# A hybrid decoder trunk on one core: ordered first loads, a router chain with fewer steps, and matrices loaded behind other readers

## The chip, the cores and the metric

One core of a Trainium2 chip. The metric is the device time of one launch in microseconds (us), the median of the runs shown. The profile is one further execution.

## What is computed

Two layers (`DEPTH = 2`) over 256 tokens of width 1024, all float32:

```python
for l in range(DEPTH):
    h = rmsnorm(x, norm1_g[l])
    proj = h @ w_in[l]                      # 1024 x 2824
    # three mixers side by side on column groups of proj:
    # mLSTM (4 heads), block attention (8 heads), S5 state space (16 groups)
    x = x + concat(y_m, y_a, y_s) @ w_out[l]
    x = x + hierarchical_moe(rmsnorm(x, norm2_g[l]), ...)

def hierarchical_moe(x, ...):               # per token
    g = argmax(x @ w_group + b_group)       # 1 of 4 groups
    top2 of (x @ w_expert + b_expert) inside group g   # 8 experts in a group
    out = sum over both of weight * ((silu(x @ w_gate[e]) * (x @ w_up[e])) @ w_down[e])
```

Each of the 32 experts of a layer has three matrices of 1024 x 512 (2 MB each), so a layer reads 96 matrices, 201 MB. The sum over the experts is the same in whichever order tokens are gathered.

## The kernel before

**Memory.** The ring is 11 tiles of 2 MB in SBUF (`tile(t)`). Matrix n of a layer (n = 0 to 95, six for each pair of experts: gate, gate, up, up, down, down) goes to tile n mod 11. While the mixers run, the same tiles hold the six chunks of `w_in` (tiles 8, 9, 0, 1, 2, 3), `w_out` (tiles 8 and 9) and the mixers' buffers (`qk`, `conv`, `pm`, `decay4`, `so`, `vm` and others), and tile 10 holds the router's buffers (`rt`, `rv`).

**Queues.** SP issues nearly all large DMAs, in one program order, each behind the waits written ahead of it (L509 to L583): first the chunks of `w_in`, then `w_out`, then the first matrices of the layer as the mixers free their tiles (1, 2, 3, 0, 6, then 4, 5, 7 behind `s_mixm` and `s_np`, then 8, 9 behind `s_op`, the last output product), then matrix 10 behind `s_ctl`, in layer 0 ten small loads for the next layer, and from matrix 11 on each pair of loads behind `s_used` of the product that read the tile's last matrix (`tile_free`). ACT's queue starts with the constants, x, four norm gains and ten small rows. POOL issues twelve small parameter loads at the start, and again for layer 1 behind `s_ctl` (L600, L601).

**Start.** PE turns x (`turn_xs`, L1408), DVE and ACT scale it by the gain into `hT`, PE multiplies by chunk 0 (`by_feature`, L1525), then by chunk 1 and so on (`by_token`, L1531). PE waits for `s_cst` (all constants) ahead of everything and for both DMAs of chunk 0 (`s_win[0]` at 32): 1 MB in rows of 1 KB, and 32 KB in 1024 rows of 32 bytes.

**Router.** After the output product PE turns x again (L1408), computes 36 logits for each token (L1824) and keeps itself busy with products that nothing reads (`busy`, L1816). DVE picks group and experts, step by step, each group of instructions closed by a `drain` (L1282 to L1322). PE counts ranks and totals with five products (L1831 to L1835) and puts the residual into four PSUM banks (L1838). DVE finds which tokens are the first 32 of experts 0 and 1 (L1335 to L1343), writes the hit matrix (L857, L860), PE gathers their rows (L1421), ACT copies them to SBUF (L608), PE turns them (L1430), DVE scales them into `xTe` (L849) and the first pass can begin (L1468). Beside this DVE works out the slots of all tokens and the number of passes and writes them to `ctl` (`s_ctl`, L1385). Every engine loads its loop counts from `ctl`.

**Passes.** A pass handles up to 32 tokens of each of two experts: PE does the gate product (L1468), the addition of the pass before (L1440), the up product (L1468), the gather for the next pass (L1421), its turning behind ACT's copy (L1430), and the down product (L1505). A pair of experts has as many passes as its fuller expert needs.

```python
def tile_free(n):                                   # on SP
    m = n - NTILE
    if m % 2 == 0:
        c = C_PASS + 1 + m // 6
        done = sp.value_load(ctl[0:1, c:c + 1], min_val=1, max_val=L * MAXN)
        wait_apart(sp, s_used[kind_of(m)], done)
```

## Time and profile before

| | |
|---|---|
| runs, median (lowest to highest) | 1274.5 us (1273.63 to 1278.43), 3 runs |
| the profiled execution | 1275.59 us |
| its span | 1273.8 us |
| PE busy, share of the span | 1070.6 us, 84% |
| DVE, ACT, POOL busy | 460.3, 180.1, 22.4 us |
| moved by DMA | 440.16 MB, mean 346 GB/s |

The span is from the first to the last instruction; the 1.8 us between it and the execution's own time lie around the program. PE, DVE, ACT, POOL and SP are TensorE, VectorE, ScalarE, GpSimd and SyncE; a q behind a name is the engine's sequencer, which issues DMAs. A float32 matmul appears as two instructions. Matmuls are pipelined, so a busy PE isn't PE at its peak. Idle time of an engine that isn't the bottleneck costs nothing.

### The profile page before, as it was taken

How to read it: one execution, taken by the hardware profiler on the slowest of the kernel's cores; microseconds unless marked ns; L12 is line 12 of the kernel's file. 1: busy time of each engine (PE TensorE's matmuls, PEld its weight loads, DVE VectorE, ACT ScalarE, POOL GpSimd, SP SyncE). 2: the span in 40 equal slices, each digit the busy share in tenths (PEclk: the TensorE clock that was granted, in tenths of full speed). 3: DMA queues.
4: the chain of work that ended last, by engine and by line, in shares of the span. 5: the costliest groups of instructions: out<-in, count | busy, mean ns of one | idle time of the engine just before them, and what ended most of it. 6: DMA issues, size and time to landing. Idle time of an engine off the chain costs nothing.

```text
span 1273.8 us, 22730 instructions
## 1 busy us (share of the span) xinstructions
PE 1070.6 (84%) x9476; PEld 578.6 (45%) x9476; DVE 460.3 (36%) x1253; ACT 180.1 (14%) x427; POOL 22.4 (2%) x34
## 2 busy tenths in 40 slices
PE   5999999999967777776799999899677777679977
PEld 4476655454533333333355755554333333334533
DVE  0786345433322222222247753533222222224331
ACT  2314310010100000000024161100000000000100
POOL 3000002000000000000000000000000000000000
PEclk9999999999988888888899999999888888889998
DMA  9711379999999999999993313899999999997996
GB/s 313 261 71 67 132 291 355 389 428 426 430 427 427 425 428 429 427 427 427 391 339 141 133 67 132 353 387 428 427 427 427 426 428 427 428 427 327 427 426 278
DMA packets 50660, 440.16 MB, mean 346 GB/s; under 512 B 9320, under 2 KB 12040, under 8 KB 25488
## 3 DMA queue, kind: packets, MB, share of 16 engines
q1 hardware_dynamic: 48672, 436.33, 83.1%
q0 software_dynamic: 800, 0.99, 0.5%
q10 hardware_dynamic: 1104, 1.59, 0.4%
q8 instruction: 69, 1.13, 0.4%
q14 instruction: 15, 0.12, 0.0%
HBM read 437.31 MB, written 1.05 MB: 344 GB/s over the span
## 4 chain that ended last, share of the span: by engine, by line
PE 55%; DMA 40%; DVE 2%; issue 1%; DVEq 1%; ACT 0%; ACTq 0%; SPq 0%
DMA ring<-in_e_w_up_dram 39%; PE PS L1468 12%; PE PS L1531 9%; PE PS L1505 7%; PE PS L1767 4%; PE PS L1430 4%; PE PS L1421 4%; PE PS L1525 3%; PE PS L1440 2%; PE PS L1701 1%; PE PS L1721 1%; PE PS L1481 1%; DMA gT<-in_norm_g_dram 1%; PE PS L1657 1%; PE PS L1824 1%
## 5 line engine op out<-in xcount | busy, mean ns | idle before, releaser
L1468 PE MATMUL PS<-ring,hT 128*32 128x256 f32 x4608 | 336.6, 452 | 164.1 <-DMA ring<-in_e_w_gate_dram 107.7
L1468 PEld LDWEIGHTS PS<-ring,hT 128*32 128x32 f32 x4608 | 181.8, 125 | 339.6 <-issue 275.9
L1505 PE MATMUL PS<-ring,hT 128*32 128x512 f32 x1152 | 134.2, 607 | 8.5 <-issue 8.2
L880 DVE TENSOR_SCALAR hT<-hT 128x256 f32<-128x256 f32 x36 | 11.0, 306 | 302.4 <-ACT hT L613 302.4
L1531 PE MATMUL PS<-ring,hT 128*128 128x512 f32 x256 | 114.8, 602 | 0.0
L1430 PE MATMUL PS<-cst,ring 64*64 64x64 f32 x1216 | 81.2, 282 | 5.8 <-ACT ring L608 1.4
L1430 PEld LDWEIGHTS PS<-cst,ring 64*64 64x64 f32 x1216 | 77.0, 212 | 15.1 <-issue 11.9
L887 DVE TENSOR_TENSOR hT<-hT,PS 128x256 f32<-128x256 f32 x36 | 15.2, 422 | 174.7 <-PE PS L1468 174.7
L1421 PE MATMUL PS<-xres,scr 128*64 128x512 f32 x304 | 73.6, 605 | 0.0
L1531 PEld LDWEIGHTS PS<-ring,hT 128*128 128x128 f32 x256 | 48.1, 193 | 54.7 <-issue 54.6
L608 ACT COPY ring<-PS 128x512 f32<-128x512 f32 x38 | 22.3, 587 | 352.6 <-PE PS L1421 352.6
L1440 PE MATMUL PS<-hT 64*128 64x512 f32 x288 | 71.8, 615 | 0.0
L1505 PEld LDWEIGHTS PS<-ring,hT 128*32 128x32 f32 x1152 | 36.0, 111 | 77.1 <-issue 75.4
L882 DVE RECIPROCAL hT<-hT 128x256 f32<-128x256 f32 x36 | 63.1, 1753 | 2.6
L1767 PE MATMUL PS<-ring 128*128 128x512 f32 x128 | 58.1, 602 | 1.9 <-DVE ring L1268 1.9
L618 ACT COPY hT<-PS 128x512 f32<-128x512 f32 x36 | 21.1, 586 | 215.5 <-PE PS L1505 215.5
L613 ACT ACTIVATE hT<-PS 128x256 f32<-128x256 f32 x36 | 13.8, 384 | 266.3 <-PE PS L1468 266.3
L849 DVE TENSOR_TENSOR hT<-PS,gT 128x512 f32<-128x512 f32 x38 | 26.3, 692 | 69.0 <-PE PS L1430 69.0
L1525 PE MATMUL PS<-hT,ring 128*128 128x256 f32 x192 | 44.9, 394 | 2.3 <-ACT hT L631 2.3
L889 DVE COPY hT<-PS 128x256 f32<-128x256 f32 x36 | 15.3, 425 | 74.8 <-PE PS L1485 74.8
L1525 PEld LDWEIGHTS PS<-hT,ring 128*128 128x128 f32 x192 | 37.8, 199 | 8.7 <-issue 3.4
L1440 PEld LDWEIGHTS PS<-hT 64*128 64x128 f32 x288 | 25.5, 186 | 32.4 <-issue 32.4
(341 smaller groups left out, 901.9 us busy)
## 6 DMA issues: line engine op xcount, KB each, us to landing
ring<-in_e_w_gate_dram SPq DMA_DIRECT2D x64, 2048.0 KB, 41.2
ring<-in_e_w_up_dram SPq DMA_DIRECT2D x64, 2048.0 KB, 44.0
ring<-in_e_w_down_dram SPq DMA_DIRECT2D x60, 2048.0 KB, 42.7
ring<-in_w_in_dram SPq DMA_DIRECT2D x10, 2048.0 KB, 18.8
ring<-in_w_out_dram SPq DMA_DIRECT2D x2, 4096.0 KB, 13.1
ring<-in_e_w_down_dram SPq DMA_DIRECT2D x8, 1024.0 KB, 39.5
...
```

Source lines behind the costliest of these rows:

```text
L608: act.copy(rows_g, PS[:, 0, :]).then_inc(gs, 1)
L618: act.copy(Y, PS[:, 3, :]).then_inc(s_ys, 1)
L849: V.tensor_tensor(xTe, PS[:, 0, :].rearrange("p (k s) -> p k s", k=KD), bcast(gT[:, l, 1, :], PAIR), ALU.mult).then_inc(xte, 1)
L882: V.reciprocal(es, es)
L1421: last = pe.matmul(PS[64 * h:64 * h + 64, 0, :], hit[:, j, :], xres[:, j, 512 * h:512 * h + 512], start=j == 0, stop=j == NT - 1)
L1430: last = pe.matmul(PS[r, 0, PAIR * k:PAIR * k + PAIR], rows_g[r, k::KD], ident[r, r], start=True, stop=True)
L1440: pe.matmul(PS[:, 4 + 2 * j + h, :], hitT[r, j, :], Y[r, :], start=False, stop=False)
L1468: last = pe.matmul(PS[o:o + UT, bank, 0:256], xTe[:, k, UT * u:UT * u + UT], w[u][:, k, :, 2 * h:2 * h + 2], start=k == 0, stop=k == KD - 1)
L1505: last = pe.matmul(PS[o:o + UT, 3, :], hTe[:, c % 2, hc:hc + UT], w[u][:, c, 512 * h:512 * h + 512], start=c == 0, stop=c == KF - 1)
L1525: last = pe.matmul(PS[:, bank, T * half:T * half + T], wchunk(c)[:, k, col:col + P], hT[:, k, :], start=k == 0, stop=k == KD - 1)
L1531: last = pe.matmul(PS[:, bank, :], hT[:, k, P * j:P * j + P], wchunk(c)[:, k, 0:512], start=k == 0, stop=k == KD - 1)
L1767: last = pe.matmul(PS[:, OUT_BANK[n], :], mixT[:, k, P * j:P * j + P], wout[:, k, 512 * h:512 * h + 512], start=k == 2, stop=k == 1)
```

## The change

Three parts.

**First loads.** ACT's queue now issues the first norm gain, the identity (the first 128 columns of the constants), x, chunk 0 of `w_in`, and the rest of the constants. SP issues the ten small rows of group 0, waits for x, then chunks 1 to 5, the other three gains and the rest. POOL's parameters wait for x too. PE and ACT wait for the identity, the gain and the rest of the constants where they use them, and PE runs four products on ones that DVE writes at the start.

**Router.** The group logits are written straight to their padded buffer, the argument of the group's exponentials is written one step later, the ranks need two products (a zero block ahead of the masks, `mks`, gives both token halves at once) and the totals two more behind them, the first hits are found with two steps in place of five, and three of the four residual products take the place of the filler products. `ctl` is written before the slots of all tokens; the slots and the weights come after `xTe`, and end in a new semaphore `s_rtd`. ACT copies the gathered rows block by block (`by_feature` to `by_block`: it now reads PSUM at a stride of 8 elements and PE reads SBUF without one), for the first pair in two halves, and PE turns them in halves in two banks, behind `s_ctl` and its own loads from `ctl`; the gate product waits for the second half before its fifth step. The copy of every later pass reads PSUM in the same way.

**Matrices.** Matrix 7 is issued behind `s_dp` (the last decay product), 5 behind `s_pm`, 4 behind `s_hmT`; matrix 10 behind `s_rtd`, with the ten small loads behind it.

The diff, cut (lines of context left out; what it removes of the second half of DVE's routing stands in the kernel above, L1324 to L1385):

```diff
-    for c0, n in CH[c]:
-        sp.dma_start(wchunk(c)[:, :, a:a + n], at(win_v, l)[0, :, :, c0:c0 + n]).then_inc(s_win[c], 16)
-        a += n
-for c in range(6):
-    load_chunk(c, 0)
+load_small(sp, 0, (0,))
+sp.wait_ge(s_x, 16)
+for c in range(1, 6):
+    load_chunk(sp, c, 0)
+for l, gi in ((0, 1), (1, 0), (1, 1)):
+    load_gain(sp, l, gi).then_inc(s_gain, 16)
...
     load_matrix(l, 6)
-    sp.wait_ge(s_mixm, l + 1)
+    sp.wait_ge(s_dp, MH * l + MH)
+    load_matrix(l, 7)
+    sp.wait_ge(s_pm, MH * l + MH)
+    load_matrix(l, 5)
+    sp.wait_ge(s_hmT, l + 1)
     load_matrix(l, 4)
-    load_matrix(l, 5)
-    sp.wait_ge(s_np, MH * l + MH)
-    load_matrix(l, 7)
...
     load_matrix(l, 9)
-    wait_apart(sp, s_ctl, l + 1)
...
 def _(pool):
+pool.wait_ge(s_x, 16)
...
         if n == 0:
-            act.wait_ge(s_gain, 32 * L)
+            act.wait_ge(s_gain0, 16)
+        elif n == 1:
+            act.wait_ge(s_gain, 16 * (2 * L - 1))
...
     act.drain()
+    if n == 0:
+        act.wait_ge(s_cst, 16)
...
-act.dma_start(cst[:, :], consts[:, 0:NC]).then_inc(s_cst, 16)
+load_gain(act, 0, 0).then_inc(s_gain0, 16)
+act.dma_start(cst[:, 0:C_MQK], consts[:, 0:C_MQK]).then_inc(s_id, 16)
 act.dma_start(xres[:, :, :], x_v).then_inc(s_x, 16)
...
-load_small(act, 0, (0,))
+load_chunk(act, 0, 0)
+act.dma_start(cst[:, C_MQK:], consts[:, C_MQK:NC]).then_inc(s_cst, 16)
 act.preload_act_table_set("natural_log_exp_and_others")
-act.wait_ge(s_cst, 16)
...
     act.activation(dif, dif, ACT.Exp).then_inc(s_rve, 1)
-    rows_gathered(s_gath0, s_gs0, l)
+    act.wait_ge(s_gath0, l + 1)
+    for c in range(2):
+        act.copy(by_block(rows_g)[:, 4 * c:4 * c + 4, :], by_feature(PS[:, 0, :])[:, 4 * c:4 * c + 4, :]
+                 ).then_inc(s_gs0, 1)
...
 V = nc.vector
+V.memset(mixT[:, 0:2, :].rearrange("p k t -> p (k t)"), 1.0).then_inc(s_warm, 1)
...
     n = 2 * l + gi
-    dve.wait_ge(s_gain, 32 * L)
+    if n == 0:
+        dve.wait_ge(s_gain0, 16)
+    else:
...
+    V.memset(gl8, -3.0e38)
+    V.memset(mks[:, 0, :], 0.0)
+    V.drain()
...
     for j in range(NT):
-        V.scalar_tensor_tensor(lg[:, j, :], PS[:, 0, 64 * j:64 * j + 36], rs[:, j:j + 1], rb[:, :], ALU.mult,
-                               ALU.add)
-    V.memset(gl8, -3.0e38)
-    V.drain()
-    V.tensor_copy(gl8[:, :, 0:4], lg[:, :, 0:4])
+        V.scalar_tensor_tensor(gl8[:, j, 0:4], PS[:, 0, 64 * j:64 * j + 4], rs[:, j:j + 1], rb[:, 0:4],
+                               ALU.mult, ALU.add)
+    for j in range(NT):
+        V.scalar_tensor_tensor(lg[:, j, :], PS[:, 0, 64 * j + 4:64 * j + 36], rs[:, j:j + 1], rb[:, 4:36],
+                               ALU.mult, ALU.add)
...
         V.max_index(idx[:, 0, j, :], gmx[:, j, :], gl8[:, j, :])
-    V.tensor_tensor(pex, lg[:, :, 0:4], gmx[:, :, 0:1].broadcast_to([P, NT, 4]), ALU.subtract).then_inc(s_rg, 1)
...
     V.tensor_tensor(elp, gid, gsel.broadcast_to([P, NT, NE]), ALU.not_equal)
-    V.drain()
-    V.scalar_tensor_tensor(elp, elp, NEG, lg[:, :, 4:36], ALU.mult, ALU.add)
+    V.tensor_tensor(pex, gl8[:, :, 0:4], gmx[:, :, 0:1].broadcast_to([P, NT, 4]), ALU.subtract).then_inc(s_rg, 1)
+    V.drain()
+    V.scalar_tensor_tensor(elp, elp, NEG, lg, ALU.mult, ALU.add)
...
     V.tensor_copy(eid, idx[:, 1, :, 0:2])
-    dve.wait_ge(s_rge, l + 1)
-    V.tensor_reduce(pgs, pex, X, ALU.add)
-    V.drain()
-    V.reciprocal(pgs, pgs)
+    V.drain()
...
     V.drain()
-    V.tensor_tensor(mks, mk[:, 0], mk[:, 1], ALU.add).then_inc(s_mk, 1)
+    V.tensor_tensor(mks[:, 1:], mk[:, 0], mk[:, 1], ALU.add).then_inc(s_mk, 1)
+    V.memset(Y, 0.0)
+    V.memset(hitT, 0.0)
+    V.drain()
+    ranks = PS[:, 1, 0:64].rearrange("p (j n) -> p j n", j=NT)
+    dve.wait_ge(s_rk, l + 1)
+    V.scalar_tensor_tensor(fsh, ranks[:, :, 0:2], 1.0, mks[:, 1:, 0:2], ALU.add, ALU.mult)
+    V.drain()
+    for j in range(NT):
+        for u in range(2):
+            last = V.tensor_scalar(hit[:, j, UT * u:UT * u + UT], cst[:, C_T + 1:C_T + 1 + UT], fsh[:, j, u:u + 1],
+                                   rs[:, j:j + 1], ALU.is_equal, ALU.mult)
+    last.then_inc(s_hit0, 1)
+    dve.wait_ge(s_cn, l + 1)
+    nf = nu.rearrange("p i u -> p (i u)")
+    V.tensor_scalar(nf, PS[:, 2, 0:NE], 1.0, 1.0 / UT, ALU.max, ALU.mult)
+    V.tensor_copy(rnk, ranks)
+    V.drain()
+    V.tensor_scalar(nf, nf, 31.0 / 64, ROUND, ALU.add, ALU.add)
+    V.tensor_scalar(fr32, rnk, 1.0 / UT, -31.0 / 64, ALU.mult, ALU.add)
+    V.drain()
+    V.tensor_scalar(nf, nf, -ROUND, None, ALU.add)
+    V.drain()
+    V.tensor_tensor(npass, nu[:, :, 0], nu[:, :, 1], ALU.max)
+    V.drain()
+    V.tensor_tensor_scan(pend, cst[:, C_ONES:C_ONES + NPAIR], npass, 0.0, ALU.mult, ALU.add)
+    V.tensor_copy(ctl[:, C_NP:C_NP + NPAIR], npass[0:1, :])
+    V.tensor_copy(c_p0, past[:, 0:1])
+    V.drain()
+    V.tensor_scalar(upr, pend[0:1, :], past[:, 0:1], None, ALU.add)
+    V.tensor_copy(c_tot, pend[0:1, NPAIR - 1:NPAIR])
+    V.drain()
+    V.tensor_copy(ctl[:, C_PASS + 1:C_PASS + 1 + NPAIR], upr).then_inc(s_ctl, 1)
+    V.tensor_copy(past[:, 0:1], upr[:, NPAIR - 1:NPAIR])
+    for c in range(2):
+        dve.wait_ge(s_rT0, 2 * l + c + 1)
+        V.tensor_tensor(xTe[:, 4 * c:4 * c + 4, :], PS[:, (3, 0)[c], 0:256].rearrange("p (k s) -> p k s", k=4),
+                        bcast(gT[:, l, 1, 4 * c:4 * c + 4], PAIR), ALU.mult).then_inc(s_xte0, 1)
+    V.tensor_scalar(fr32, fr32, ROUND, -ROUND, ALU.add, ALU.add)
+    V.tensor_tensor(pst[:, :, 0], pend, npass, ALU.subtract)
+    V.drain()
+    V.scalar_tensor_tensor(rnk, fr32, float(UT), rnk, ALU.mult, ALU.add)
+    V.tensor_scalar(pst[:, :, 1], pst[:, :, 0], float(PAIR), float(UT), ALU.mult, ALU.add)
+    V.tensor_scalar(pst[:, :, 0], pst[:, :, 0], float(PAIR), None, ALU.mult)
+    V.drain()
+    V.tensor_tensor(rnk, rnk, rv[:, 160:192].unsqueeze(1).broadcast_to([P, NT, NE]), ALU.add)
+    dve.wait_ge(s_rge, l + 1)
+    V.tensor_reduce(pgs, pex, X, ALU.add)
+    V.drain()
+    for a in range(2):
+        V.tensor_tensor(rtm[:, a], mk[:, a], rnk, ALU.mult)
+    V.reciprocal(pgs, pgs)
...
     V.drain()
+    V.tensor_reduce(sh.rearrange("p a j -> p (a j)"), rtm.rearrange("p a j n -> p (a j) n"), X, ALU.add)
...
     V.drain()
+    V.tensor_copy(sw, sh)
...
     V.drain()
-    V.tensor_tensor(wgt[:, :, 1:2], wgt[:, :, 0:1], dif, ALU.mult)
-    V.memset(Y, 0.0)
-    V.memset(hitT, 0.0)
...
+    V.tensor_tensor(wgt[:, :, 1:2], wgt[:, :, 0:1], dif, ALU.mult).then_inc(s_rtd, 1)
+    V.drain()
...
-    pe.wait_ge(s_xte0, l + 1)
+    pe.wait_ge(s_xte0, 2 * l + 1)
...
 pe.sem_inc(s_xte, 1)
-pe.wait_ge(s_cst, 16)
+pe.wait_ge(s_warm, 1)
+warm = mixT[:, 0:2, :].rearrange("p k t -> p (k t)")
+for n in range(4):
+    pe.matmul(PS[:, 4 + n % 2, :], warm[:, 0:P], warm, start=True, stop=True)
+pe.wait_ge(s_id, 16)
...
         for k in range(KD):
+            if kind == 0 and k == KD // 2:
+                pe.wait_ge(s_xte0, 2 * l + 2)
...
-    def busy(n):
-        for k in range(n):
-            pe.matmul(PS[:, 4 + 2 * (k % 2), :], ident, cst[:, 0:512], start=True, stop=True)
     turn_xs(l, 1)
-    busy(1)
...
-    busy(4)
+    def residual(n):
+        pe.matmul(PS[:, 4 + n, :], ident, xres[:, n // 2, 512 * (n % 2):512 * (n % 2) + 512], start=True, stop=False)
+    for n in range(3):
+        residual(n)
     pe.wait_ge(s_mk, l + 1)
+    flat_mks = mks.rearrange("p j n -> p (j n)")
     bef = cst[:, C_BEFORE:C_BEFORE + P]
-    pe.matmul(PS[:, 1, 0:NE], bef, mks[:, 0, :], start=True, stop=True)
-    pe.matmul(PS[:, 1, NE:2 * NE], ones, mks[:, 0, :], start=True, stop=False)
-    pe.matmul(PS[:, 1, NE:2 * NE], bef, mks[:, 1, :], start=False, stop=True)
-    pe.matmul(PS[:, 1, 2 * NE:3 * NE], ones, mks[:, 0, :], start=True, stop=False)
-    pe.matmul(PS[:, 1, 2 * NE:3 * NE], ones, mks[:, 1, :], start=False, stop=True).then_inc(s_rk, 1)
-    for j in range(NT):
-        for h in range(2):
-            pe.matmul(PS[:, 4 + 2 * j + h, :], ident, xres[:, j, 512 * h:512 * h + 512], start=True, stop=False)
+    pe.matmul(PS[:, 1, 0:2 * NE], bef, flat_mks[:, NE:3 * NE], start=True, stop=False)
+    pe.matmul(PS[:, 1, 0:2 * NE], ones, flat_mks[:, 0:2 * NE], start=False, stop=True).then_inc(s_rk, 1)
+    pe.matmul(PS[:, 2, 0:NE], ones, mks[:, 1, :], start=True, stop=False)
+    pe.matmul(PS[:, 2, 0:NE], ones, mks[:, 2, :], start=False, stop=True).then_inc(s_cn, 1)
+    residual(3)
...
     gather(s_gath0)
-    pe.wait_ge(s_gs0, l + 1)
-    turn_gathered(s_rT0)
-    wait_apart(pe, s_ctl, l + 1)
+    pe.wait_ge(s_ctl, l + 1)
+    passes = pe.value_load(ctl[0:1, C_NP:C_NP + 1], min_val=1, max_val=MAXN // 2)
+    past_n = pe.value_load(ctl[0:1, C_PASS:C_PASS + 1], min_val=0, max_val=L * MAXN)
+    for c in range(2):
+        pe.wait_ge(s_gs0, 2 * l + c + 1)
+        for k in range(4 * c, 4 * c + 4):
+            for h in range(2):
+                r = slice(64 * h, 64 * h + 64)
+                last = pe.matmul(PS[r, (3, 0)[c], PAIR * (k % 4):PAIR * (k % 4) + PAIR],
+                                 by_block(rows_g)[r, k, :], ident[r, r], start=True, stop=True)
+        last.then_inc(s_rT0, 1)
```

## Rows read from the trace of the kernel before

**Rows 1.** The page, 40 slices: GB/s

```profile
GB/s 313 261 71 67 132 291 355 389 428 426 430 427 427 425 428 429 427 427 427 391 339 141 133 67 132 353 387 428 427 427 427 426 428 427 428 427 327 427 426 278
```

**Rows 2.** Timeline 0 to 60: start, us, engine, line, operation, idle before and releaser

```profile
9.96 3.65 PE L1408 MATMUL PS<-cst,xres 128*128 128x128 f32 x16 [9.96 <-DMA xres<-in_x_dram]
...
13.80 1.06 ACT L628 ACTIVATE scr<-xres 128x1024 f32<-128x1024 f32 x1 [4.50 <-DMA gT<-in_norm_g_dram]
...
17.27 9.39 PE L1525 MATMUL PS<-hT,ring 128*128 128x256 f32 x32 [1.44 <-ACT hT L631]
```

**Rows 3.** DMA issues of the whole run: KB each, median us to landing

```profile
cst<-in_consts_dram ACTq DMA_DIRECT2D x1, 484.5 KB, 3.6
```

**Rows 4.** Line L521, the issue at 1.5 us (second DMA of chunk 0)

```profile
DMA to landing us min/median/max: 14.7/14.7/14.7
```

**Rows 5.** DMA queues from 5 to 8 us: packets, MB, share (q10 ACT, q1 SP)

```profile
q10 hardware_dynamic: 218, 0.83, 70.9%
q1 hardware_dynamic: 218, 0.22, 21.3%
```

**Rows 6.** DMA queues from 16 to 26 us

```profile
q1 hardware_dynamic: 1937, 3.90, 105.1%
```

**Rows 7.** The chain that ended last, 70 to 90 us

```profile
79.34 6.91 PE PS L1525 x32
```

**Rows 8.** Timeline of PE, 340 to 392 us

```profile
378.46 6.24 PE L1468 MATMUL PS<-ring,hT 128*32 128x256 f32 x64 [5.67 <-DMA ring<-in_e_w_gate_dram]
...
388.48 3.83 PE L1468 MATMUL PS<-ring,hT 128*32 128x256 f32 x64 [1.86 <-DMA ring<-in_e_w_up_dram]
```

**Rows 9.** Timeline 172 to 225, layer 0: router chain to the first pass

```profile
190.66 0.23 DVE L1322 TENSOR_TENSOR ring<-ring 128x64 f32<-128x64 f32 x1
...
192.08 3.68 PE L1838 MATMUL PS<-xres,cst 128*128 128x512 f32 x8
...
192.41 0.10 DVE L1336 TENSOR_TENSOR ring<-PS,cst 128x4 f32<-128x4 f32 x1
...
194.32 0.29 DVE L860 TENSOR_TENSOR scr<-scr 128x128 f32<-128x128 f32 x1
...
195.69 1.94 PE L1421 MATMUL PS<-xres,scr 128*64 128x512 f32 x8
...
197.67 0.59 ACT L608 COPY ring<-PS 128x512 f32<-128x512 f32 x1 [7.67 <-PE PS L1421]
...
198.31 2.14 PE L1430 MATMUL PS<-cst,ring 64*64 64x64 f32 x32 [0.69 <-ACT ring L608]
...
199.09 0.15 DVE L1385 CAST ctl<-ring 1x16 int32<-1x16 f32 x1
199.27 0.33 SPq L516 DMA_DIRECT2D ring<-in_e_w_down_dram  x1
...
200.82 0.69 DVE L849 TENSOR_TENSOR hT<-PS,gT 128x512 f32<-128x512 f32 x1 [1.58 <-PE PS L1430]
...
201.76 3.83 PE L1468 MATMUL PS<-ring,hT 128*32 128x256 f32 x64 [1.32 <-DVE hT L849]
...
203.72 0.25 SPq L477 DMA_DIRECT2D small<-in_s_glu_b_dram  x1
```

**Rows 10.** Line L516, issue at 205.7 us (matrix 11)

```profile
DMA to landing us min/median/max: 11.7/11.7/11.7
```

**Rows 11.** Line L516, issue at 241.1 us (matrix 17)

```profile
DMA to landing us min/median/max: 8.1/8.1/8.1
```

**Rows 12.** Window: PE, PEld, DVE, ACT, POOL busy, PEclk, DMA share, GB/s

```profile
206.00:212.00 6.00, 6.00 (x76) 2.63 (x74) 3.33 (x4) 0.04 (x1) 1.81 (x3) 1.00 1.05 273
```

**Rows 13.** Timeline 804 to 845, layer 1: matrices 10 and 11, first pass

```profile
824.65 8.12 SPq L516 DMA_DIRECT2D ring<-in_e_w_down_dram  x2
...
826.88 5.46 PE L1468 MATMUL PS<-ring,hT 128*32 128x256 f32 x64 [1.41 <-DVE hT L849]
```

**Rows 14.** Line L516, issues at 832.4 and 832.8 us (matrices 11, 12, layer 1)

```profile
DMA to landing us min/median/max: 8.1/10.3/12.6
```

More of the change, by code:

```diff
@@ L323, in build @@
         s_rk = sem("ranks_ready")
+        s_cn = sem("counts_ready")
         s_ctl = sem("units_ready")
+        s_rtd = sem("routing_buffers_read")
         s_out = sem("stored")
@@ L860, in row_hits @@
                 V.tensor_tensor(hit, hit3[:, 0], hit3[:, 1], ALU.add).then_inc(ready, 1)
-            def hits(ready):
-                row_hits(ready, iota, sh)
                 V.tensor_scalar(sh, sh, -float(PAIR), None, ALU.add)
```

90 lines of the change are left out of this document (37 added, 53 removed).

## The prediction

> **What bounds the kernel.** Read the slices first [rows 1]: DMA runs at 427 GB/s for most of the time and is nearly idle in two valleys, while the mixers run. The ring holds 11 matrices, so outside the valleys the time is bytes by rate: a 2.1 MB matrix takes 2.1/0.427 = 4.9 us. So three things can shorten it: a mixer that begins earlier, less idle DMA between a mixer and the steady stream, or fewer small packets within it. A faster instruction elsewhere is worth nothing.
>
> **The start.** In the timeline [rows 2] PE turns x from 9.96 (it waited for x). ACT starts only at 13.80, held by the norm gains, the first product starts at 17.27 behind `hT`. From there PE leads the chain through the mixer, so what the first product gains, the mixer's end and all behind it gain. Two more things are to be seen. Both queues progress packet for packet: 218 against 218 between 5 and 8 us [rows 5], although ACT's are four times as large. And the first product is slow: 9.39 us, where the same 32 instructions take 6.91 later [rows 7], so 2.5 are lost to a slow clock. After 5.67 us of idling a gate product took 6.24 us, after 1.86 only 3.83 [rows 8].
>
> *x.* The constants, first in the queue, landed 3.6 us after issue [rows 3]: 0.5 MB at 390 GB/s (3.90 MB in 10 us [rows 6]) is 1.3, so 2.3 go before the data flows. x, 1.05 MB, takes 2.7; issued third at about 1.7, overlapping that latency, it lands at some 6.4 (now 9.96, when PE went on [rows 2]). ACT's square (1.06) and scalings, and PE's turning (3.65 [rows 2]) bring `hT` to about 11.
>
> *Chunk 0.* Its second DMA, 1024 rows of 32 bytes, landed at 1.5 + 14.7 = 16.2 [rows 4], so it was barely hidden already. Now its first DMA runs alone behind x (1.05 MB, 2.8 us, to 9.2), but SP issues chunk 1 when x lands, and that reaches the engines at 9.2 or a little later (a lone matrix lands 8.1 us after issue, 3.2 more than its 4.9 [rows 11]). From then the tiny rows alternate with 2 KB packets, which go at 1937/10 = 194 in a us [rows 6]. If all 1024 alternate, 5.3 us and their own cost: landing at 15.5 to 17.5, POOL's small packets included. If a good part slips ahead, 12 to 13. I take 14.3, between them, since chunk 1 can't begin earlier than SP's wait allows. The product starts at 14.5: 2.8 earlier. Of the 2.5 of slow clock I take 0.8 back: PE idles 3 to 4 us between its turning and the product, between the two gaps of [rows 8]. **Start: -3.6**, bounds +1 (17.5 and more, no clock) and -8.7 (`hT` at 11 leads, clock kept). The rest of the constants comes behind chunk 0, at about 17; first needed by the scales, long ahead of the product on ones after the gate columns. Covered by the first product; uncovered it would cost what it is late. Chunks 1 to 5 keep their rate and are used later than they land.
>
> **The router, layer 0** [rows 9]. Masks ready at 190.9. The copy, one reduction, one reciprocal and two drains leave the path, two narrow logit writes come in: -0.35, to 190.55. Ranks need two products before their signal in place of five, each pair 0.22: ready at 191.4 (DVE resumed at 192.4). The clearing of `Y` and `hitT`, between L1322 and L1336, now lies beside them. First hits: DVE took 2.2 us (192.4 to 194.6); two steps and four writes take 1.3, to 192.7. The residual products, which held the gather until 195.69 although the hits were there at 194.61, are done by then, as three ran while DVE chose experts. Gather at 192.8 (-2.9), done at 194.75. The path to `ctl`: 14 groups took 4.5 us behind the hits (to 199.1), 0.32 each; seven are left: 195.0. PE then loads its counts. No row shows that by itself; DVE went from 199.24 to 200.82 with two such loads and a wait for PE that ended at 200.45, so it lies between 0 and 1.6; I take 1.2, near the upper end, since DVE started late after its releaser. Turning 196.2 to 198.4 (2.14), second half of `xTe` 198.8. The pass starts at 198.4 in place of 201.76: -3.4.
>
> That isn't what the time follows, though. Matrix 10, issued at 199.27, now waits for `s_rtd`: seven groups, 15 instructions, behind `xTe`, 2.8 us by the same price (bounds 2.3 and 3.3): 201.6, so it is issued 2.4 **later**. Queued behind it on SP are ten small loads (the last issued at 203.72, 0.25 us: 4.7 us in all after matrix 10) and only then the wait for tile 0: matrix 11 is issued at about 206.3 (now 205.7), though the gate product ends at 202.3. Matrix 10 alone would land at 209.7, 11 at 214.6. POOL's small loads wait for `ctl` alone, as matrix 10 did, and start some 4.2 us earlier. They cost the stream dearly: 273 GB/s from 206 to 212 [rows 12] is (427-273) x 6/427 = 2.2 us, and matrix 11 landed 11.7 after issue [rows 10] in place of 8.1. Moved ahead they fall half into time in which DMA idles: 1.6 us of loss are left, 11 lands at 216.2 (now 217.4), matrix 16 at 241.2. Matrix 17 was issued at 241.1 only (pair 1 needs two passes) and landed 8.1 later [rows 11], at 249.2. With the passes 3.4 ahead it is issued at 237.7, and lands behind 16: 246.2. I take **-2.6** for layer 0, bounds 0 and -3.4 (the passes' own lead). From there DMA is never idle, and the layer's end moves with it.
>
> **Layer 1** [rows 13]. Matrix 10 was issued at 824.65, 11 at 832.43 behind the gate product, and landed 8.1 later, at 840.5 (the first of the two in [rows 14]). Now 10 at 827.1, landed 835.2, 11 behind it 840.1; the gate product (at the latest 829) isn't last any more. **-0.4**, bounds +1 and -2.
>
> **Matrices 4, 5, 7.** They move ahead by 1 to 10 us, but 8 and 9 still wait for the last output product, and 10 for the router. The stream then idles for some 10 us ahead of matrix 10. Worth nothing: what the first pass reads has landed anyhow. SP's waits in front of them end in the order written. The filler products take no time that anyone waits for; their cover, keeping PE's clock, is taken by residual products.
>
> **The strided copy.** ACT copies 512 columns in 0.59 us in each pass [rows 9]; no row shows PSUM read at a stride. PE has transposes to do while it runs (the first copy of a layer has no such cover). I take no change; at twice the price it adds 0.5 us in the last pass of each layer and in the first ones; below zero nothing, as it reads the same bytes.
>
> The Trainium skill ("SBUF — State Buffer", section "Door 1: The DMA port swizzle") says that PSUM comes in lines of 8 bytes and that "any non-contiguous PSUM access pattern significantly slows down matmuls". It names no figure for a copy. By it the sum would be smaller by some 1 to 2 us; no row here shows it.
>
> **Sum:** -3.6 - 2.6 - 0.4 = -6.6. The profiled execution took 1275.6 and comes to 1269.0; against the median of 1274.5, 1.1 below it, 1267.9. Half a per cent (6.4 us) is about what a measurement of this kernel can tell from no change.
>
> **Rivals.**
> *A, the tiny rows stay last.* Chunk 0 lands at 16.5 to 18, the start gives 0 to 0.8. For it: 218 against 218. Against: its first DMA has 2.8 us alone behind x. Then -0.5 - 2.6 - 0.4: 1271.0. Chance 0.27. The Trainium skill ("DMA: Bandwidth & Descriptors", section "Rules for kernel authors") says that spreading DMAs over queues doesn't help bandwidth, as all share 16 engines; by that, only the order counts, which would be this case.
> *B, chunk 0 lands by 11 and PE keeps its clock.* Start -8, sum -11: 1263.5. For it: the rows of 32 bytes are small. Against: the gap of 5.67 in [rows 8]. Chance 0.16.
> *C, slower: matrix 10 behind a longer chain.* If the strided halves cost three times their 0.59/2 and the loads from `ctl` 1.6, `s_rtd` comes 2.5 us later still: 10 lands at 837.7 in layer 1, 11 at 842.6 (+2.1), in layer 0 the small loads and 11 slip by as much (0 left of the gain), the last passes add 1 each, and if the start gives nothing either the sum is +4: 1278.5. It decides from `s_rtd` later than 827.4 in layer 1. For it: the stream idles in both layers at this point. Chance 0.07.
> That the change doesn't do what it says at the start, since another of PE's waits (`s_par`) ends as late, would look like A and is in its chance.
>
> **Chances.** The forecast 0.5; C 0.07, A 0.27, B 0.16. Of the forecast's own spread (1264 to 1271) some two thirds lie beyond -6.4: faster 0.33 + 0.16 + 0.02 = 0.51; same 0.17 + 0.25 + 0.01 = 0.43; slower 0.06. The range takes A in and most of B: 1261.5 to 1273.5.
>
> **What would show it.** Right: x landed by 6.5, first product at 13 to 16; first pass 3 to 4 us earlier after the logits; matrix 10 issued later after the logits than now, matrix 17 issued before 16 has landed; DMA idle before matrix 10; matrices 4, 5, 7 earlier without effect. Wrong: chunk 0's second DMA the last before the product and later than 17, a copy L608 over 0.8 us, or matrix 11 of layer 1 landing longer after its matrices 8 and 9 were issued than now.

## The result, and the profile after

The kernel after takes 1261.2 us (median of 4 runs, 1258.8 to 1264.6); before, run beside it, takes 1276.5 (1273.6 to 1286.9). **The ratio is 0.9873, interval 0.9848 to 0.9898.** The same file measured once more, later, gave 0.9900 (0.9872 to 0.9929); the two say 16 and 13 us faster. The forecast was 6.6 us faster, 1267.9, with a range down to 1261.5: the sign was right, and the gain was at least twice as large.

The profiled execution took 1264.6 (span 1262.8, 11.0 below that of before). DMA of the page in 40 slices, and the granted clock:

```profile
PEclk9999899999988888888899999899888888789988
...
GB/s 308 275 103 55 119 390 271 428 426 428 426 429 424 429 427 429 426 427 429 381 343 141 134 67 206 261 417 427 427 426 427 427 427 428 428 426 362 428 427 284
```

The shape is that of [rows 1], with the two valleys. Outside them the slice that stands out is the fourth from the right, late in layer 1: it was 327 and is 362. Nothing in the prediction touched it.

**The start.** Timeline of the kernel after (start, length, engine, line, operation, count, idle before):

```profile
6.94 2.03 PE L1437 MATMUL PS<-cst,xres 128*128 128x128 f32 x16
...
9.29 2.15 ACT L653 ACTIVATE hT<-PS,gT 128x128 f32<-128x128 f32 x8
...
11.69 8.83 PE L1560 MATMUL PS<-hT,ring 128*128 128x256 f32 x32 [2.04 <-ACT hT L653]
```

The first product waits for ACT's half of `hT`, not for chunk 0, and starts at 11.69 in place of 17.27 [rows 2]. Where chunk 0's two DMAs (1 KB rows, then the 1024 rows of 32 bytes) landed, by the issues of their line:

```profile
L521 ACTq DMA_DIRECT2D ring<-in_w_in_dram x2: 637/659/681, 2.1 to 2.8; - x2
...
DMA to landing us min/median/max: 7.6/7.7/7.9
```

Issued at 2.15 and 2.81, landed at 10.0 and 10.4: the tiny rows landed only 0.4 us behind the large ones.

**The router, layer 0**, same view (it answers to [rows 9]):

```profile
178.94 3.81 PE L1854 MATMUL PS<-rw,hT 128*128 128x36 f32 x32 [0.27 <-ACT hT L653]
...
192.99 1.15 PE L1883 MATMUL PS<-cst,ring 64*64 64x64 f32 x32 [1.62 <-ACT ring L838]
...
194.39 3.88 PE L1499 MATMUL PS<-ring,hT 128*32 128x256 f32 x64 [0.25 <-DVE hT L1387]
...
197.28 0.33 SPq L536 DMA_DIRECT2D ring<-in_e_w_down_dram  x1
```

From the end of the logits (182.75; before 186.04) to the first pass it is 11.6 us in place of 15.7. Matrix 10 is issued at 197.28, 14.5 behind the logits in place of 13.2. Matrix 17, which ends the stage for DMA:

```profile
L536 SPq DMA_DIRECT2D ring<-in_e_w_down_dram x1: 340/340/340, 231.8 to 231.8; - x1
...
DMA to landing us min/median/max: 11.8/11.8/11.8
```

It lands at 243.6. Counted from the turning of x for the router (176.57; before 179.46) that is 67.1 us in place of 69.7. In layer 1:

```profile
816.85 3.83 PE L1499 MATMUL PS<-ring,hT 128*32 128x256 f32 x64 [0.25 <-DVE hT L1387]
...
819.99 1.52 SPq L536 DMA_DIRECT2D ring<-in_e_w_down_dram  x2
```

Both issues stand in one row: 10 at 819.99, 11 at 821.19. Matrix 11 no longer waits for the gate product but queues behind 10, and lands at 833.5 (before 840.5 [rows 14]).

**The turning of the gathered rows**, which the prediction had used as a duration and not as a term. Groups by line (busy us, mean ns of one; before, the group also holds the first pass of each layer, which the kernel after has on a line of its own). First before:

```profile
L1430 PE MATMUL PS<-cst,ring 64*64 64x64 f32 x1216 | 81.2, 282 | 5.8 <-ACT ring L608 1.4
L1430 PEld LDWEIGHTS PS<-cst,ring 64*64 64x64 f32 x1216 | 77.0, 212 | 15.1 <-issue 11.9
L608 ACT COPY ring<-PS 128x512 f32<-128x512 f32 x38 | 22.3, 587 | 352.6 <-PE PS L1421 352.6
```

Then the kernel after:

```profile
L1459 PE MATMUL PS<-cst,ring 64*64 64x64 f32 x1152 | 41.3, 220 | 4.4
L1459 PEld LDWEIGHTS PS<-cst,ring 64*64 64x64 f32 x1152 | 37.4, 134 | 11.9 <-issue 11.9
L628 ACT COPY ring<-PS 128x512 f32<-128x512 f32 x36 | 21.1, 585 | 324.9 <-PE PS L1450 324.9
```

Per pass, 32 of these took 2.14 us and now take 1.15. The weights of the products are the gathered rows: before, PE loaded every 8th column (`rows_g[r, k::KD]`), now a contiguous block. ACT reads at the stride instead, and its copy took 585 ns against 587.

### The profile page after: what moved, and what is told of

It reads as the page before. It is cut to its first block, busy times and chain, and to the rows that moved or that the text cites. A ratio compares the mean times of both kernels' runs of the same rounds, so it can differ in the third digit from the quotient of the medians.

```text
span 1262.8 us, 22686 instructions
## 1 busy us (share of the span) xinstructions
PE 1041.1 (82%) x9460; PEld 546.6 (43%) x9460; DVE 458.5 (36%) x1246; ACT 180.0 (14%) x429; POOL 22.3 (2%) x34
## 4 chain that ended last, share of the span: by engine, by line
PE 52%; DMA 43%; issue 2%; DVE 1%; ACT 1%; ACTq 1%; SPq 0%; DVEq 0%
DMA ring<-in_e_w_up_dram 36%; PE PS L1499 11%; PE PS L1566 9%; PE PS L1536 6%; PE PS L1803 5%; DMA ring<-in_e_w_gate_dram 4%; PE PS L1560 3%; PE PS L1450 3%; DMA ring<-in_e_w_down_dram 3%; PE PS L1459 2%; PE PS L1469 2%; PE PS L1737 1%; PE PS L1757 1%; PE PS L1512 1%; PE PS L1693 1%
## 5 line engine op out<-in xcount | busy, mean ns | idle before, releaser
L1499 PE MATMUL PS<-ring,hT 128*32 128x256 f32 x4608 | 340.6, 456 | 171.8 <-DMA ring<-in_e_w_gate_dram 124.9
L1499 PEld LDWEIGHTS PS<-ring,hT 128*32 128x32 f32 x4608 | 185.6, 126 | 348.1 <-issue 287.8
L906 DVE TENSOR_SCALAR hT<-hT 128x256 f32<-128x256 f32 x36 | 10.6, 294 | 346.1 <-ACT hT L633 345.8
L1536 PEld LDWEIGHTS PS<-ring,hT 128*32 128x32 f32 x1152 | 38.3, 112 | 95.9 <-issue 94.9
L1803 PE MATMUL PS<-ring 128*128 128x512 f32 x128 | 60.8, 625 | 1.9 <-DVE ring L1293 1.9
L1459 PE MATMUL PS<-cst,ring 64*64 64x64 f32 x1152 | 41.3, 220 | 4.4
L1459 PEld LDWEIGHTS PS<-cst,ring 64*64 64x64 f32 x1152 | 37.4, 134 | 11.9 <-issue 11.9
L1803 PEld LDWEIGHTS PS<-ring 128*128 128x128 f32 x128 | 24.9, 201 | 29.1 <-issue 26.3
```

Of the source, the lines that this page charges most:

```text
L1459: last = pe.matmul(PS[r, 0, PAIR * k:PAIR * k + PAIR], by_block(rows_g)[r, k, :], ident[r, r], start=True, stop=True)
L1499: last = pe.matmul(PS[o:o + UT, bank, 0:256], xTe[:, k, UT * u:UT * u + UT], w[u][:, k, :, 2 * h:2 * h + 2], start=k == 0, stop=k == KD - 1)
L1536: last = pe.matmul(PS[o:o + UT, 3, :], hTe[:, c % 2, hc:hc + UT], w[u][:, c, 512 * h:512 * h + 512], start=c == 0, stop=c == KF - 1)
L1803: last = pe.matmul(PS[:, OUT_BANK[n], :], mixT[:, k, P * j:P * j + P], wout[:, k, 512 * h:512 * h + 512], start=k == 2, stop=k == 1)
```

## The experiments

One table serves all of them. It cuts the profiled execution of each kernel at events on the path, in us: from the first product's start (F) to the first turning for the router (T0), to matrix 17's landing, and so on; "starved" is the time between the landings of layer 1's matrices 76 and 77 (the 175th and 176th expert load, as two matrices of a layer come in halves), "last" from the last landing to the end.

| kernel | F | mixer 0 | T0 to 17 | last load to layer 1 | mixer 1 | T1 to 17 | starved | last |
|---|---|---|---|---|---|---|---|---|
| before | 17.3 | 162.2 | 69.7 | 10.4 | 159.1 | 65.7 | 10.5 | 11.3 |
| after | 11.7 | 164.9 | 67.1 | 9.2 | 159.0 | 64.6 | 8.1 | 10.3 |
| turning back | 11.7 | 161.5 | 67.3 | 9.2 | 161.0 | 63.3 | 10.6 | 11.3 |
| turning alone | 18.0 | 160.8 | 68.3 | 9.2 | 160.1 | 65.8 | 8.0 | 10.3 |
| start back | 18.4 | 165.3 | 66.8 | 9.8 | 165.3 | 63.3 | 7.8 | 10.3 |
| start, turning | 11.8 | 159.6 | 69.6 | 9.8 | 159.1 | 64.0 | 7.8 | 9.3 |
| chunk 1 early | 21.4 | 162.8 | 67.2 | 9.2 | 164.1 | 63.6 | 7.8 | 10.3 |
| tiny rows first | 13.5 | 163.0 | 67.2 | 9.4 | 159.1 | 64.5 | 7.9 | 9.3 |
| no warm-up | 12.3 | 163.5 | 66.8 | 9.7 | 165.3 | 63.5 | 9.3 | 9.3 |
| after again | 12.0 | 161.6 | 67.7 | 9.2 | 164.2 | 63.7 | 8.3 | 10.2 |
| order back | 11.7 | 160.4 | 66.7 | 9.8 | 159.1 | 64.8 | 8.3 | 10.3 |
| filler back | 12.1 | 160.4 | 67.4 | 9.2 | 159.0 | 64.7 | 8.0 | 10.3 |
| own buffers | 11.7 | 159.9 | 64.3 | 9.2 | 160.9 | 59.4 | 8.1 | 10.3 |
| own buffers, small loads | 11.8 | 160.4 | 64.0 | 9.2 | 160.8 | 59.4 | 8.0 | 10.3 |

The parts left out are the same in all: 386.3 to 386.5 from matrix 17 to layer 0's last load, 291.7 to 291.8 from 17 to 76 in layer 1, 89.5 to 89.8 from 77 to the end of the loads. That is the stream whose time is bytes by rate. Both mixers vary by up to 6 us between executions and follow no edit that one profile each can show. The other columns also move by 0.5 to 1.5 us where no edit touches them, so a difference of that size in one row shows nothing by itself.

### The turning back, and the turning alone

```diff
-                act.copy(by_block(rows_g), by_feature(PS[:, 0, :])).then_inc(gs, 1)
+                act.copy(rows_g, PS[:, 0, :]).then_inc(gs, 1)
-                        last = pe.matmul(PS[r, 0, PAIR * k:PAIR * k + PAIR], by_block(rows_g)[r, k, :], ident[r, r], start=True,
+                        last = pe.matmul(PS[r, 0, PAIR * k:PAIR * k + PAIR], rows_g[r, k::KD], ident[r, r], start=True,
```

> The kernel after, with the passes' copy and turning as before: ACT copies the gathered rows as they lie, PE turns every 8th column (the first pass of a layer keeps the new form, since its halves are copied apart). Theory T (contiguous weights shorten each pass by 1 us where a pass is on the path: end of layer 0 1.0, a starved stretch late in layer 1 2.3, last pass 1.1): the turning group takes 2.1 us again in place of 1.15, and the time is 4.4 us above the kernel after, 1265.6, ratio to before 0.9915. Rival (the turning lies beside the stream of matrices and is worth nothing; the eleven microseconds are start and router): the group is slower but the time stays at 1261.2, ratio 0.988.

Measured: ratio 0.9919 (0.9891 to 0.9946), 1266.0 us. That is 2 us above the kernel after by its second ratio and 6 by its first, and the intervals of all three overlap: the time alone doesn't settle it. Its groups:

```profile
L1459 PE MATMUL PS<-cst,ring 64*64 64x64 f32 x1152 | 76.9, 282 | 4.4
L1459 PEld LDWEIGHTS PS<-cst,ring 64*64 64x64 f32 x1152 | 73.0, 212 | 12.0 <-issue 12.0
```

Where it counts is seen around the starved stretch. Windows (us, PE busy, clock, DMA share, GB/s), first of before:

```profile
1150.00:1160.00 10.00, 9.87 (x120) 1.00 0.87 369
1160.00:1170.00 10.00, 10.00 (x147) 1.00 0.47 167
```

after:

```profile
1150.00:1160.00 10.00, 10.00 (x146) 1.00 0.63 228
1160.00:1170.00 10.00, 9.88 (x132) 1.00 1.01 429
```

and with the turning back:

```profile
1140.00:1150.00 10.00, 9.88 (x120) 1.00 0.86 367
1150.00:1160.00 10.00, 10.00 (x148) 1.00 0.49 169
```

A pair with three passes keeps its matrices three passes long, and SP issues no load meanwhile: DMA has landed all it was given and waits, PE is full. Before, matrix 77 was issued at 1164.8, 2.4 us after 76 had landed at 1162.4; after, at 1154.4, 0.3 before 76 landed. With the turning back the gap is there again (issue at 1154.65, 76 landed at 1152.3).

The gap has two causes, though, and the turning is one. In the first of the three passes the down product was slow in both kernels that show the gap of 2.4, and fast in the kernel after. Before, then after:

```profile
1138.07 5.27 PE L1505 MATMUL PS<-ring,hT 128*32 128x512 f32 x32 [1.24 <-issue]
```

```profile
1130.36 3.64 PE L1536 MATMUL PS<-ring,hT 128*32 128x512 f32 x32 [0.52 <-issue]
```

The run without the warm-up (below) has the new turning and that slow product:

```profile
1134.99 5.30 PE L1535 MATMUL PS<-ring,hT 128*32 128x512 f32 x32 [2.15 <-issue]
...
L536 SPq DMA_DIRECT2D ring<-in_e_w_down_dram x1: 328/328/328, 1160.7 to 1160.7; - x1
```

The granted clock was 0.83 there from 1130 to 1140, and 1.00 in the kernel after. Matrix 76 had landed at 1159.4, so the gap was 1.3: at the same slow product, the turning closes 1.0 of the 2.4, and "starved" is 9.3 in place of 10.5. The rest goes with the clock. Both kernels with the old turning had the slow product and eleven of the twelve with the new one had not; whether the shorter turning or chance moves the slow stretch is open.

The other place is the last pass, after:

```profile
1250.81 1.15 PE L1459 MATMUL PS<-cst,ring 64*64 64x64 f32 x32
1251.89 3.64 PE L1536 MATMUL PS<-ring,hT 128*32 128x512 f32 x32
```

and with the turning back:

```profile
1250.95 2.14 PE L1459 MATMUL PS<-cst,ring 64*64 64x64 f32 x32
1253.02 3.64 PE L1536 MATMUL PS<-ring,hT 128*32 128x512 f32 x32
```

So by the columns the turning is worth 1.2 + 1.0 = 2.2 us with the clock taken out, and 3.4 with it. The expectation had put 1.0 more at the end of layer 0, and that fell: "last load to layer 1" is 9.2 with the turning back too. ("Last" is 9.3 in three runs with the new turning: there the granted clock stayed at full in the 14 us before the last load landed, where it fell to half for 3.4 us in all the others.)

> The kernel before, with the copy by blocks and the turning of contiguous columns alone, nothing else changed. Theory T: 4.4 us below before, 1272.1, ratio 0.9965, turning group 1.15 us, ACT copy of 512 columns still 0.59 us. Rival (off the path): 1276.5, ratio 1.000.

Measured: 0.9976 (0.9958 to 0.9993), 1274.0 beside 1277.5 of before. The group is at 1.15 us, the copy at 585 ns, starved 8.0, last 10.3. The rival (worth nothing) is out by the interval, narrowly, and by both columns; the size is 3 us by the ratio, 1 to 5 by its interval. Here the turning also counts in layer 0: matrix 17 waits for the passes there, and from the end of the first gate product to its issue it is 33.5 us in place of 35.5. In the kernel after, 17 is issued before 16 has landed, and "T0 to 17" is the same with the turning back. So the worth of the parts doesn't add up, and of the 2.7 that "T0 to 17" fell from before to after, the turning alone gives 1.4.

### The start

> The kernel after, with the loads at the start in the order of before (constants ahead of x, the norm gains behind it, all chunks on SP) and without the four products on ones. Theory S (what the first product gains is kept to the end): first product at 17.3 us, time 6.1 above the kernel after, 1267.3, ratio 0.9928. Rival G (the mixer gives 3.4 us of it back by a lower granted clock at 130 to 160 us, as in the one profile of the kernel after, whenever it begins earlier): 2.7 above, 1263.9, ratio 0.990.

Edit: the `load_*` calls of the three DMA queues in the order of before, and no products on ones. Measured: 0.9938 (0.9919 to 0.9956), 1270.0. First product at 18.4, a microsecond later than before, as x landed at 12.8 and not at 9.8. The time is 5 to 8 us above the kernel after by its two ratios, for a first product 6.7 us later: theory S. Both mixers took 165.3 here, though they began late, so rival G's dip needs no early beginning. The first product took 7.15 us, with the loads of before and no warm-up:

```profile
18.36 7.15 PE L1552 MATMUL PS<-hT,ring 128*128 128x256 f32 x32 [0.49 <-ACT hT L648]
```

> The kernel before, with the new start and the new copy and turning, but the router, its residual products and the order of matrices 4, 5, 7 as before. Theory (start 6.1, turning 4.4, all kept but for dips of the clock that fall differently in each run): 1276.5 - 10.5 = 1266.0, ratio 0.992, and what is left to the kernel after, 3 to 5 us, is the router's. Rival G (2.7 for the start): 1269.4, ratio 0.9945, and the router is worth 8.

Measured: 0.9924 (0.9903 to 0.9945), 1267.2. What is left to the kernel after is 0.0024 to 0.0051 by its two ratios, 3 to 6 us, as the theory had it; the columns "T0 to 17" and "T1 to 17" say some 2 and nothing. With the router of before this run has 64.0 in layer 1, as short as the new router's 63.3 to 64.8. Its gate product there:

```profile
818.40 3.83 PE L1492 MATMUL PS<-ring,hT 128*32 128x256 f32 x64 [0.98 <-DVE hT L874]
```

Before took 5.46 [rows 13] and the turning alone 5.43, and these two have the 65.7 and 65.8: that a new router shortens layer 1 isn't shown.

> The kernel after, unchanged. Theory D (the mixers' length varies from execution to execution with the granted clock, by up to 5 us, and the profile of the kernel after had caught a dip in layer 0): the time from the first product to the turning of x for the router, 164.9 us in that profile, is between 159 and 165, the stream of matrices behind it repeats to 0.3 us, ratio to before 0.987 to 0.990. Rival (the new kernel always pays 3.4 us in layer 0's mixer): again 164.9 within 0.5.

Measured: 0.9900 (0.9872 to 0.9929), 1265.7 beside 1278.2. The mixer of layer 0 took 161.6 and not 164.9; layer 1's took 164.2 and not 159.0. Windows over 130 to 150 us, first of the kernel after, then again:

```profile
130.00:150.00 20.00, 20.00 (x70) 0.80 0.07 17
```

```profile
130.00:150.00 20.00, 20.00 (x81) 0.95 0.16 50
```

The granted clock was 0.80 there in the one and 0.95 in the other, the same program. Theory D holds: the dip in the first profile of the kernel after, which hid 2.7 us of its gain (F to T0 took 164.9 against 162.2 of before), belongs to the execution.

### Chunk 0 and its tiny rows

Edit: SP does not wait for x before chunks 1 to 5.

```diff
             load_small(sp, 0, (0,))
-            sp.wait_ge(s_x, 16)
```

> The kernel after, with SP not waiting for x before chunks 1 to 5: chunk 1 is issued at about 4.6 us in place of 6.8. Theory I (a row of 32 bytes takes a turn of its own beside each 2 KB packet of another queue, and in the kernel after they were only spared because chunk 1 was not yet flowing): chunk 0's second DMA lands at 14 us or later in place of 10.4, the first product starts 3 us later, 1264.5, ratio to before 0.990. Rival (the tiny rows are cheap even beside other packets): lands by 12, first product by 12.5, time within 1 us of the kernel after, 0.988.

Measured: 0.9958 (0.9937 to 0.9979), 1274.3, which is 7 to 11 us above the kernel after. The same view of chunk 0's two DMAs, and the first product:

```profile
L521 ACTq DMA_DIRECT2D ring<-in_w_in_dram x2: 637/659/681, 2.1 to 2.8; - x2
...
DMA to landing us min/median/max: 9.2/13.8/18.5
```

and in the timeline

```profile
21.41 9.46 PE L1559 MATMUL PS<-hT,ring 128*128 128x256 f32 x32 [11.74 <-DMA ring<-in_w_in_dram]
```

The tiny rows landed at 2.8 + 18.5 = 21.3, 11 us later than in the kernel after, for an issue of chunk 1 that was 2.0 us earlier. Theory I has the mechanism and undershot the size. Chunk 1 itself (1024 rows of 2 KB, on SP's queue) landed at 18.0, so the 1024 tiny rows were spread over the whole of it and the beginning of chunk 2: one of theirs for each large one, as the 218 against 218 of [rows 5] had it. The queues from 11 to 13 us here (packets, MB, share), then ACT's in the kernel after from 9 to 10:

```profile
q1 hardware_dynamic: 302, 0.62, 88.0%
...
q10 hardware_dynamic: 301, 0.01, 10.7%
```

```profile
q10 hardware_dynamic: 971, 0.24, 133.2%
```

That is 150 tiny rows in a microsecond beside the large ones, and over 870 where only ACT's queue moved.

In the second variant ACT also issues the tiny rows ahead of the 1 KB rows:

> As the run in which SP issues chunk 1 without waiting for x (there chunk 0's 1024 rows of 32 bytes landed at 21.3 us), but ACT issues the rows of 32 bytes ahead of chunk 0's rows of 1 KB. Theory I (what counts is how many rows take a turn beside the 2 KB packets, whatever their size, and the tiny ones now go before chunk 1 flows): the tiny rows land by 9 us, the 1 KB rows, alternating with chunk 1, by 13 to 16, the first product starts by then and not at 21.4; time 0.991 to 0.993 of before. Rival (chunk 1 takes the engines whatever the order): both land at 20 or later, first product at 20, ratio 0.9955.

Measured: 0.9905 (0.9873 to 0.9937), 1264.3.

```profile
L521 ACTq DMA_DIRECT2D ring<-in_w_in_dram x2: 637/659/681, 2.1 to 2.8; - x2
...
DMA to landing us min/median/max: 5.8/8.2/10.6
```

and in the timeline

```profile
13.53 9.76 PE L1558 MATMUL PS<-hT,ring 128*128 128x256 f32 x32 [3.60 <-DMA ring<-in_w_in_dram]
```

The tiny rows landed at 7.9, 0.8 us behind x, and the 1 KB rows, now those that share the engines with chunk 1, at 13.4. Theory I again, in both landings (the ratio came out a little better than the 0.991 to 0.993 expected, within its interval). So the 32-byte rows cost what stands beside them, not what they carry.

The Trainium skill says in "DMA: Bandwidth & Descriptors", section "Queues, rings and completion order", that each DMA engine goes round the queues it has work for, a packet at a time. The trace agrees: 301 packets of ACT's queue went beside 302 of SP's.

### The products on ones

> The kernel after, without the four products on ones ahead of the identity. Theory W (they matter only through PE's clock in the first turning): the turning of x takes 3.6 us in place of 2.0, the first product starts 1 to 2 us later, time 1.5 above the kernel after, ratio 0.9885. Rival (they also carry the clock into the first product): that product takes 9.4 or more in place of 8.8, and the time is 2.5 above.

Measured: 0.9892 (0.9852 to 0.9932), 1266.6.

```profile
7.13 3.65 PE L1436 MATMUL PS<-cst,xres 128*128 128x128 f32 x16 [7.13 <-DMA xres<-in_x_dram]
```

The turning took 3.65 again, in place of 2.03, as theory W said, but the product started at 12.3, only 0.6 later in place of 1 to 2: ACT's scalings of `hT` are the last to end. It took 8.67, in this one profile. With the warm-up the same product took 7.14 four times and 8.8 four times where it began by 12.1, so nothing shows what the warm-up does for it. The time can't be told from the kernel after's.

### Order of matrices 4, 5, 7, and the filler

> The kernel after, with matrices 4, 5, 7 issued in the order and behind the waits of before. Theory O (worth nothing, as matrices 8 and 9 and then 10 wait for later events and DMA idles between them): the time from the turning of x for the router to the landing of matrix 17 is 67.0 us in layer 0 as in the kernel after, ratio 0.987 within its interval. Rival (matrices 8 and 9 land later and hold up the first pass's up product or push matrix 10): 17 lands a microsecond or more later after the turning, ratio above 0.989.

Measured: 0.9899 (0.9861 to 0.9936), 1263.3, the ratio of the repeated kernel after; T0 to 17 is 66.7, no later. Worth nothing that can be told, as theory O had it.

> The kernel after, with one filler product (512 columns) put back between the turning of x and the router's products. Theory F (it is on the path since hT is ready as soon as the turning ends, contrary to the prediction's sentence on fillers): the router's products end 6.6 us after the turning began, as before, in place of 6.2, in both layers. Rival (DVE's and ACT's copies of hT hide it, as predicted): 6.2, unchanged.

Measured, one run, which says nothing of the time: 1260.7. The timeline shows the filler, two entries of 1.02 us together, between the turning (at 172.51) and the logits:

```profile
174.45 1.02 PE L1850 MATMUL PS<-cst 128*128 128x512 f32 x2
175.31 3.94 PE L1855 MATMUL PS<-rw,hT 128*128 128x36 f32 x32
```

The logits end 6.7 us after the turning began (6.1 in the repeated kernel after), and the first pass starts 18.4 after it and not 17.8. In layer 1 they end at 6.5, between the 6.7 and 6.1 of the two profiles of the kernel after, so layer 0 alone supports it. Theory F holds there: the filler was on the router's path. Yet "T0 to 17" is 67.4, within what the kernel after gives (67.1 and 67.7), so its 0.6 us did not reach the stream that can be told.

### The router's buffers outside the ring

In the kernel after, matrix 10 waits for `s_rtd`, because the router's buffers lie in its tile. Here they lie in the idle part of hT and of the scratch:

```diff
-        rt = so[:, :, :].rearrange("p j n -> p (j n)")
-        rv = vm[:, 0:512]
+        rt = work[:, 1536:2048]
+        rv = scr[:, 640:1024]
+        rs8 = scr[:, 384:400]
+        rmk = scr[:, 400:496]
...
                 load_matrix(l, 9)
-                sp.wait_ge(s_rtd, l + 1)
                 load_matrix(l, 10)
+                wait_apart(sp, s_ctl, l + 1)
...
+                act.wait_ge(s_rtd, l + 1)
                 wait_apart(act, s_ctl, l + 1)
```

(`rs8` and `rmk` hold `gl8` and `mks`; their clearing comes behind the wait for `s_rs`.)

> The kernel after, with the router's buffers outside the ring (the idle part of hT and of the scratch), so that matrix 10 is issued right behind 8 and 9 and waits for no router; ACT waits for the router's last step ahead of its first pass. Theory B (in the kernel after matrix 10, issued only when the router ends, sets when matrix 11 lands in layer 1, and POOL's small loads and the gate product do in layer 0): matrix 10 lands by 196 in layer 0; 11 is issued when the first gate product ends; layer 1's matrix 11 lands 8.1 us after issue, 4 us earlier; layer 0 gains 0.5 to 2. Time 5 below the kernel after, 1256.2, ratio to before 0.9835. Rival (the passes' own speed sets layer 1, DMA soon catches up with the last readers of the ring): no more than 1 below the kernel after, 0.987.

Measured: **0.9822 (0.9791 to 0.9853), 1255.8 us**, 6 to 10 us below the kernel after by its two ratios. Matrix 11's issue in layer 0 and in layer 1:

```profile
L538 SPq DMA_DIRECT2D ring<-in_e_w_down_dram x1: 350/350/350, 193.4 to 193.4; - x1
...
DMA to landing us min/median/max: 11.2/11.2/11.2
...
L538 SPq DMA_DIRECT2D ring<-in_e_w_down_dram x1: 328/328/328, 813.6 to 813.6; - x1
...
DMA to landing us min/median/max: 8.8/8.8/8.8
```

In layer 1 it lands 8.8 after issue in place of 12.3, and T1 to 17 falls from some 64 to 59.4; in layer 0 T0 to 17 falls from 67 to 64.3. Theory B, with the 5 us it gave come out at 7: matrix 10 landed at 190.5 in layer 0 (by 196 expected), and layer 0 gained 2.8 or more (0.5 to 2 expected).

> As the run with the router's buffers outside the ring, and the next layer's small loads (SP's behind matrix 10, POOL's behind the logits) are issued while DMA is idle under the router. Theory B2 (the small packets cost the stream about 1.6 us where they lie beside matrices 11 and 12): layer 0's matrix 11 lands 8.1 us after issue in place of 9.9; 1.5 to 2 us below the run with the buffers alone, 1254.5, ratio 0.982. Rival (their cost is hidden since the passes set the pace at that point): equal to that run.

Measured: 0.983 (0.9798 to 0.9862), 1256.1: equal to the run before, so the rival holds. Matrix 11 does land 8.5 us after issue in place of 11.2:

```profile
L538 SPq DMA_DIRECT2D ring<-in_e_w_down_dram x1: 350/350/350, 194.5 to 194.5; - x1
...
DMA to landing us min/median/max: 8.5/8.5/8.5
```

But T0 to 17 gains 0.3 only: matrix 17 can't be issued before the second pass of its pair, and was at 228.0, 0.8 us before 16 landed.

## Why the prediction was right and wrong

By the two profiles, the 11.0 us of span are: start -5.6, mixer 0 +2.7, router of layer 0 -2.7, end of layer 0 -1.2, router of layer 1 -1.1, starved stretch -2.3, last pass -1.0, and +0.2 in the streams. Without the mixer, whose length belongs to the execution, that is -13.7, or 0.989 of before, between the two measured ratios. Three more of these parts are not the edit's alone: about half of the starved stretch goes with a lower clock, the 1.2 at the end of layer 0 are there with the turning back too, and the 1.1 of layer 1 are there with the router of before (64.0 in "start, turning"). That the total comes out between the ratios doesn't show the parts.

**What bounds the kernel.** "Outside the valleys the time is bytes by rate" holds for 768 us of the span and fails in the slice of 327 GB/s of [rows 1], which lay in plain view; no reason for it was sought. "A faster instruction elsewhere is worth nothing" was drawn from it, and **this is the step that failed**: the pass sets the pace behind a pair with three passes and at the end, and a shorter turning counts there. It put at nothing what made the time 3 us shorter when it was done alone (1 to 5 by its interval).

**The strided copy.** The sum took "no change" for ACT's side, which was right (585 ns against 587), and stopped there. The other side of the same edit, PE reading contiguous weights in place of every 8th column, was never priced, although [rows 9] had the 2.14 us for 32 products and the sum used them for the new kernel's first pass too. The sentence of the Trainium skill that the prediction quotes ("SBUF — State Buffer", section "Door 1: The DMA port swizzle") is about matmuls. For ACT's copy the trace shows no such price: it reads 512 columns at a stride of 8 in the same time.

For the weights, the trace has 212 ns a load at a stride of 8 and 134 ns contiguous, 64 columns. The Trainium skill gives in "TensorE: Matmul & The Clock Gate", section "LDWEIGHTS (loading the stationary operand)", a time that follows from the number of columns and names no stride; by that both would be equal, and the measurement decides against it.

**The start.** This is the other step that failed, by size: -3.6 was forecast (2.8 of beginning, 0.8 of clock), -6.1 came (5.58 and 0.56). x landed at 6.80 (6.4 forecast), ACT's half of `hT` was ready at 11.45 (11 forecast). The term that was mis-sized is chunk 0's landing, 14.3 forecast, 10.4 measured. The mechanism was right, that tiny rows alternate with whatever else flows; when chunk 1 begins to flow was wrong. SP issued it at 6.82, and its first packet came 3.7 us later, at 10.5, when chunk 0 was through (9.2 or a little later forecast). The prediction's own chance for a landing by 11 was 0.16. It stands on a knife's edge: chunk 1 issued 2.0 us earlier costs 9.7 us at the first product. Of the slow clock 0.56 came back (8.83 against 9.39). In four later executions it was all of it (7.14), but so it was once with the loads of before (7.15), so this part belongs to the execution.

**The router, layer 0.** -2.6 forecast, -2.7 measured, and this is in part luck. The prediction's own landing of 17, 246.2 against 249.2, gives -3.0, of which it took 2.6. Counted from the logits, the passes lead by 4.1 us and not 3.4, and matrix 10 is late by 1.3 and not 2.4. Set against T0, matrix 11 landed at 216.6 on the clock of before (216.2 forecast) and 17 at 246.5 (246.2): 17 behind 16, as written. But 17 was issued 3 us earlier than forecast, 2.0 of them by the turning, and that didn't show only because 16 was still under way.

**Layer 1.** With the 6.6 us of lead at T1 taken off, matrix 10 was forecast to land at 828.6 and 11 at 833.5, and both did to a tenth; that 10 and no longer the gate product holds 11 was right. The tenth is luck: 10 was issued 0.5 us earlier than forecast and took 8.6 in place of 8.1, and in the repeated profile 11 landed 1.1 us sooner after T1. Between 11 and 17 it was another 0.7 less than before, for which no term and no cause is known. **Matrices 4, 5, 7**: nothing, right.

**The fillers** "take no time that anyone waits for": wrong by 0.6 us on the router's path, but without a share in the time that can be told.

**The rivals.** A (tiny rows last) fell, though two microseconds at SP's issue separate it from the truth. B was nearest to the time, 1263.5, with chunk 0 landed by 11 as it says, but it reached the number without the turning and with a clock that this profile didn't keep. C fell: `s_rtd` was early enough (826.6 on the clock of before, against 827.4, a narrow margin). The range ended 0.3 us above the measurement because a part of the edit had no term: the start's own bound, -8.7, held what came.
